# RWKV scan inverse: the power W kept folded to 32 columns, turned folded on VectorE and spread with a block mask

## The reference

```python
def _wkv_step(S, inp):
    r_t, w_t, k_t, v_t, a_t, b_t = inp
    sa = jnp.einsum('zbhvk,zbhk->zbhv', S, a_t)
    S = S * w_t[..., None, :] + sa[..., :, None] * b_t[..., None, :] + v_t[..., :, None] * k_t[..., None, :]
    return S, jnp.einsum('zbhvk,zbhk->zbhv', S, r_t)

def wkv_bidir(state0, scan_in):
    state, ys = lax.scan(_wkv_step, state0, scan_in)
    ys = jnp.moveaxis(ys, 0, 2)
    return state, ys[0] + ys[1][:, ::-1]
```

## Time and profile before

| | us |
|---|---|
| median of 3 runs | 4006.78 (3999.78 to 4009.26) |
| the profiled execution | 4001.04 |
| its span, first to last instruction | 3999.2 |
| products with WR as moving operand, first to last start | 2821.5 to 3349.1 |
| busy in the whole span: PE, PEld, DVE, ACT, POOL | 3689.2, 2635.5, 2316.2, 1210.3, 1289.5 |

### The profile page before, as it was taken

The page is one execution under the profiler, slowest core; times in us unless marked ns, Lnnn a source line. Parts: engine busy times, 40 slices in busy tenths (PEclk is TensorE's granted clock), DMA queues, the critical chain, the costliest instruction groups (busy, mean ns, idle before and its releaser), DMA issues. The chain is left out here.

```text
span 3999.2 us, 76514 instructions
## 1 busy us (share of the span) xinstructions
PE 3689.2 (92%) x30402; PEld 2635.5 (66%) x30402; DVE 2316.2 (58%) x3880; ACT 1210.3 (30%) x2668; POOL 1289.5 (32%) x1004
## 2 busy tenths in 40 slices
PE   8888999898999999899999998898999999899887
PEld 6667778757787798778344444783899997633332
DVE  4568982545986345566344444767777775533333
ACT  3352222344222322332111111224455554111112
POOL 4453445434445355474000000340555552000000
PEclk9999999998999999999999999999999998899999
DMA  4214543302554132234999997255433334599997
GB/s 129 57 54 168 186 155 100 105 1 89 174 182 160 61 106 76 87 131 183 407 420 420 420 420 308 84 186 200 125 91 92 88 96 148 218 376 421 421 421 307
DMA packets 231184, 787.42 MB, mean 197 GB/s; under 512 B 56008, under 2 KB 64024, under 8 KB 171136
## 3 DMA queue, kind: packets, MB, share of 16 engines
q1 hardware_dynamic: 225008, 764.05, 51.4%
q0 software_dynamic: 5328, 19.40, 1.2%
q10 hardware_dynamic: 576, 0.09, 0.0%
HBM read 736.08 MB, written 47.38 MB: 196 GB/s over the span
## 5 line engine op out<-in xcount | busy, mean ns | idle before, releaser
L3011 ACT ACT_TABLE_LOAD x32 | 41.1, 1283 | 519.6 <-PE moe1e_p_u L2957 262.7
L2887 POOL DMA_INDIRECT moe0e_xg<-moe_h,moe_first_rows x20 | 18.9, 947 | 541.1 <-DVE moe_first_rows L3044 535.4
L1227 DVE SCALAR_TENSOR_TENSOR f0u_ada<-hT,condition,f0u_ada 128x512 f32<-128x512 f32 x168 | 189.0, 1195 | 0.4 <-DVE f0u_ada L1227 0.4
L373 POOL TENSOR_TENSOR gmi_w_lo<-gmi_rows_w,gmi_w_hi 128x512 fp32r<-128x512 f32 x64 | 120.2, 1879 | 159.5 <-ACT gmi_w_hi L415 159.5
L1227 DVE SCALAR_TENSOR_TENSOR f1u_ada<-hT,condition,f1u_ada 128x512 f32<-128x512 f32 x168 | 157.8, 1007 | 13.4 <-DMA hT<-in_ada_w_dram 12.9
L4031 PE MATMUL scan_bank<-scan_WR,scan_Z 64*64 64x96 f32 (+1 forms) x3072 | 162.3, 237 | 3.1 <-DVE scan_Z L3949 3.0
L373 POOL TENSOR_TENSOR p_w_lo<-p_rows_w,p_w_hi 128x512 fp32r<-128x512 f32 (+3 forms) x88 | 113.1, 1286 | 160.7 <-ACT p_w_hi L415 160.7
L2887 POOL DMA_INDIRECT moe1e_xg<-moe_h,moe_first_rows x17 | 16.0, 940 | 453.1 <-DVE moe_first_rows L3044 447.4
L1159 POOL TENSOR_TENSOR f0u_w_lo<-f0u_w,f0u_w_hi 128x1024 fp32r<-128x1024 f32 x42 | 114.8, 2754 | 138.0 <-ACT f0u_w_hi L1175 138.0
L1159 POOL TENSOR_TENSOR f1u_w_lo<-f1u_w,f1u_w_hi 128x1024 fp32r<-128x1024 f32 x42 | 113.7, 2726 | 139.1 <-ACT f1u_w_hi L1175 139.1
L2984 PE MATMUL moe0e_p_y<-moe_ring,moe0e_gatedT 128*64 128x512 f32 x608 | 134.7, 594 | 7.8 <-ACT moe0e_gatedT L3013 7.8
(11 more groups left out here) (912 smaller groups left out, 11363.7 us busy)
## 6 DMA issues: line engine op xcount, KB each, us to landing
moe_ring<-in_moe_w_down_dram SPq DMA_DIRECT2D x140, 1024.0 KB, 18.3
gm_uT<-in_moe_w_gu_dram SPq DMA_DIRECT2D x111, 1024.0 KB, 18.0
moe_ring<-in_moe_w_gu_dram SPq DMA_DIRECT2D x102, 1024.0 KB, 21.8
walk_memory<-in_moe_w_gu_dram SPq DMA_DIRECT2D x60, 1024.0 KB, 24.5
hT<-in_ada_w_dram SPq DMA_DIRECT2D x48, 1024.0 KB, 6.8
f0u_w<-in_ffn_w_gate_up_dram SPq DMA_DIRECT2D x22, 1024.0 KB, 4.9
f1u_w<-in_ffn_w_gate_up_dram SPq DMA_DIRECT2D x22, 1024.0 KB, 4.9
gmi_rows_w<-in_ga_w_in_dram SPq DMA_DIRECT2D x64, 256.0 KB, 2.6
```

Source lines behind the costliest of these rows:

```text
L373: nc.gpsimd.tensor_tensor(w_lo[t % 2][:, 0:width], w[t % RAW][:, 0:width], w_hi[t % 2][:, 0:width], ALU.subtract).then_inc(w_lo_made, 1)
L1227: ins = V.scalar_tensor_tensor(out=acc[:, z, :], in0=src, scalar=cond[:, n * HALF + k, z:z + 1], in1=acc[:, z, :], op0=ALU.mult, op1=ALU.add)
L2887: pool.indirect_dma_start(xg[:], None, H.h, bass.IndirectOffsetOnAxis(rows[:, 0:1], 0)).then_inc(gathered, 16)
L3011: nc.scalar.activation(sg[:], p_g[:], ACT.Silu).then_inc(silu_ready, 1)
```

## The change

W is kept folded to 32 columns too. `WR` has now 64 columns per chunk: 32 of W, 32 of the inverse. A new tile `Zt` holds folded powers.

- PE: the nine products of stages 1 to 3 have 64 moving columns and not 96.
- ACT: `copy_power` moves 128 x 128 and not 128 x 256.
- DVE, stage 0: the turn of Z (128 x 256) becomes an add of the two column halves of Z into `Zt` (128 x 128), a wait for it, and a turn of 128 x 128.
- DVE, stages 1 to 3: the turn of the power (128 x 256) becomes a turn of 128 x 128 into `Zt`, a wait for it, and a multiply of `Zt`, read twice, with the block mask, into Z (128 x 256).
- POOL: the same instruction as before, written shorter.

```diff
-        WR = sb("WR", [P, STEPS, CH + CH // 2])
+        WR = sb("WR", [P, STEPS, CH])
+        Zt = sb("Zt", [P, STEPS, CH // 2])
...
-        power, folded = slice(0, CH), slice(CH, CH + CH // 2)
+        power, folded = slice(0, CH // 2), slice(CH // 2, CH)
+
+        def spread(x):
+            return x.rearrange("p c (o t) -> p c o t", o=1).broadcast_to([P, 4, 2, CH // 2])
...
+        block_masks = join[:, 3, :].rearrange("p (q o t) -> p q o t", q=1, o=2).broadcast_to([P, 4, 2, CH // 2])
...
-                        A(WR[:, chunks(n), power], wide(n)[:, :, power], ACT.Copy).then_inc(s["z_copied"], 1)
+                        A(WR[:, chunks(n), power], one(n)[:, :, power], ACT.Copy).then_inc(s["z_copied"], 1)
...
                         if n // NG == FIRST:
                             dve.wait_ge(s["z_copied"], h * COPIED + copies_through(n))
-                            turn(WR[:, g4, power], Z[:, g4, :])
+                            V.tensor_tensor(Zt[:, g4, 0:CH // 2], Z[:, g4, 0:CH // 2], Z[:, g4, CH // 2:CH], ALU.add).then_inc(s["t_half"], 1)
+                            dve.wait_ge(s["t_half"], h * HALVED + n + 1)
+                            turn(WR[:, g4, power], Zt[:, g4, 0:CH // 2])
                         elif squares(n):
-                            turn(Z[:, g4, :], WR[:, g4, power])
+                            V.transpose(Zt[:, g4, :], WR[:, g4, power]).then_inc(s["t_half"], 1)
+                            dve.wait_ge(s["t_half"], h * HALVED + n + 1)
+                            V.tensor_tensor(by_block(Z[:, g4, :]), spread(Zt[:, g4, :]), block_masks, ALU.mult).then_inc(s["t_made"], 1)
...
-                                mm = mmul(wide(n)[:, q], stationary[:, j, :], WR[:, j, :])
+                                mm = mmul(one(n)[:, q, :], stationary[:, j, :], WR[:, j, :])
```

More of the change, by code:

```diff
@@ L3541, in rwkv_scan @@
     NI = PRODUCTS * NG
-    ADDED, COPIED, TURNED = 5 * NG, 5 * NG, 6 * NG
+    ADDED, COPIED, TURNED, HALVED = 5 * NG, 5 * NG, 6 * NG, 4 * NG
     FIRST, LAST_POWER, OUTER, FINAL = 0, 4, 5, 6
@@ L3595, in rwkv_scan @@
                  "tr_ready tr_copied t_made t1_made at_ready "
-                 "off_ready outer_ready inv_ready z_copied r_added r_folded r_full eed_made "
+                 "off_ready outer_ready inv_ready z_copied r_added r_folded r_full t_half eed_made "
                  "bon_ready bon_read bonus_done bonus_shifted km_made kh_made factor_step tables_loaded "
@@ L3618, in one @@
             return bank[INV_BANK[n % 4]][:, 0:4 * CH].rearrange("p (c t) -> p c t", c=4)
-        def wide(n):
-            return bank[INV_BANK[n % 4]][:, 0:4 * (CH + CH // 2)].rearrange("p (c t) -> p c t", c=4)
         def narrow(n):
             return bank[INV_BANK[n % 4]][:, 0:2 * CH].rearrange("p (c t) -> p c t", c=4)
-        power, folded = slice(0, CH), slice(CH, CH + CH // 2)
+        power, folded = slice(0, CH // 2), slice(CH // 2, CH)
+        def spread(x):
+            return x.rearrange("p c (o t) -> p c o t", o=1).broadcast_to([P, 4, 2, CH // 2])
         def by_block(x):
@@ L3759, in body @@
                         pool.wait_ge(s["r_added"], h * ADDED + adds_through(LAST_POWER * NG + g))
-                        nc.gpsimd.tensor_tensor(by_block(full[:, g4, :]), WR[:, g4, folded].rearrange("p c (o t) -> p c o t", o=1).broadcast_to([P, 4, 2, CH // 2]),
-                                                join[:, 3, :].rearrange("p (q o t) -> p q o t", q=1, o=2).broadcast_to([P, 4, 2, CH // 2]), ALU.mult).then_inc(s["r_full"], 1)
+                        nc.gpsimd.tensor_tensor(by_block(full[:, g4, :]), spread(WR[:, g4, folded]), block_masks, ALU.mult).then_inc(s["r_full"], 1)
                     if ahead is not None:
@@ L3961, in add_product @@
                                 dve.wait_ge(s["r_folded"], h * NG + n % NG + 1)
-                            V.tensor_tensor(WR[:, g4, folded], WR[:, g4, folded], wide(n)[:, :, folded], ALU.add).then_inc(s["r_added"], 1)
+                            V.tensor_tensor(WR[:, g4, folded], WR[:, g4, folded], one(n)[:, :, folded], ALU.add).then_inc(s["r_added"], 1)
                         elif n // NG == LAST_POWER:
```

## The result

The changed kernel takes 4026.05 us in the median of 6 runs (4022.98 to 4029.6), against 4005.43 for the kernel before (6 runs, 3999.78 to 4009.26): a ratio of 1.0053, interval 1.0040 to 1.0066. It is 21 us (0.5%) slower, which is small but clear of the interval. The prediction was 4022, with slower as the likeliest outcome.

A forecast was written before the change was run, and what follows sets the result against it. DVE's work on stage 3 was taken to set the tail and the head. 15 heads x 1.04 = 15.6 us on 4001.0 gave 4016.6 profiled, median 4022, own range 4014 to 4032, 8 in 10 3997 to 4037.

The forecast's parts named there:

- The main step: DVE in stages 0 to 3: new two-SBUF-input instructions wait for POOL, so 2.8 us of work costs 1.04 us per head.
- the sum: Whole scan: 15 heads x 1.04 = 15.6 us on 4001.0, giving 4016.6 profiled and a median of 4022.
- The prices: Stages 1 to 3: DVE's cost per unit rises from 0.56 to 0.87 us; copy and half product get shorter.
- idle time before the adds: Sign in the profile: DVE's idle time before adds of stages 1 to 3 falls from 45 to under 15 us.
- The order: Stage 1 to 3 factor parts: `kh` on POOL goes ahead of the second half of `at_rt`, add 6 at 3000.15.
- Rival 1: `at_rt` goes ahead of `kh`: add 7 some 0.6 us earlier, add 12 0.4 late, median 4013; chance 0.20.
- Add 12: DVE's add of product 12, ahead of the tail: at 3007.6 and not 3006.57, making each of 15 heads 1.04 us longer.
- Head 0: First head of the scan: counted among the 15 heads that each get 1.04 us longer.
- The last head: No factor parts, `km` or `kh`: DVE's +0.31 stands against 0.10 + 0.12 off PE and ACT, taken as 0.
- Rival 2: Stages 1 to 3: DVE keeps up, shorter products and copies count, add 12 0.7 us earlier, median 3996; chance 0.15.
- Rival 3: DVE's 128 x 128 turn is all fixed cost, 0.44 us: add 12 2.3 us late, median 4041; chance 0.06.
- Rival 4: The walk sets the head and DVE's delay hides beside it, within 3 us: median 4007; chance 0.12.

The follow-up runs named there:

- experiment 4: Changed kernel with the turned half written to free PSUM columns and the half add taking one half from PSUM: 4005.77 us, ratio 1.0000 to the kernel before.
- Experiment 5: Changed kernel with one more wait on POOL, so `kh` waits until the second half of `at_rt` is done on DVE: 4026.35 us, ratio 1.0048.
- experiments 1: Changed kernel with the products of stages 1 to 3 put back to 96 moving columns: 4030.19 us, ratio 1.0065 to the kernel before.
- Experiment 6: Changed kernel with one idle PE matmul ahead of each wait for a turn of products 10 to 14, heads 0 to 14: 4025.53 us, ratio 1.0047.
- experiment 2: Kernel before with 64-column products in stages 1 to 3 and the 128 x 128 power copy, DVE's work as before, part of W left out: 3997.64 us.
- experiment 3: Changed kernel without the block-mask multiply, the turned half going straight into Z, part of the computation left out: 3991.80 us, ratio 0.9971.

## Why the prediction was right

The main step, that both kinds of new instruction have two inputs in SBUF and so wait for whole POOL instructions, which turns work that would just fit into 1 us more per head, held at each place, and experiment 4 isolates it. Counted from the copy of the bonus, the forecast had adds 3, 6, 8 and 12 at 5.57, 12.57, 15.62 and 20.02 us; they came at 5.61, 12.47, 15.50 and 20.02. In terms of the sum:

- The prices: turn of 128 x 128 0.30, measured 0.302; multiply 0.43 alone, measured 0.425; copy 0.26, measured 0.277; half product 0.23, measured 0.24 (3001.36 to 3001.60); idle time before the adds under 15 us, measured 2.1. One price was missed: a factor part behind a multiply takes 0.03 to 0.04 us longer, from start to start, than one behind a turn (`bh` 0.43 before and 0.47 after, `at_rt` of 128 x 256 0.30 and 0.34, `rk` 0.36 and 0.39). That the chain still ends at 20.02 is partly luck, since the norm's two small ones took 0.34 and not 0.42 and other adds came 0.1 early.
- The order: `kh` went in ahead of `at_rt`, as forecast with a margin of 0.06 us. Rival 1 put a price of 0.6 us on this order. Experiment 5 made that order and won 0.1: a `kh` that starts later also ends later, and the next multiply waits for that end. Since its semaphore itself delays `kh` by up to 0.37 us (0.22 behind against 0.15 ahead), how much of the rival's 0.6 was to be had stays open. The prediction calls this rival the second where it speaks of the order of issue; it is rival 1.
- Add 12 was forecast 1.04 late. It is 1.31 late (18.71 to 20.02). In the head that I read, add 12 already stood 0.28 later than in the others (18.99), which is that difference: in that head it came 1.03 later. The head as a whole got 1.33 longer. 14 x (1.33 - 1.04) = 4 us were missed here.
- Head 0 was counted like the others, 1.0, and got 6.1. It has no walk, and in the trace before DVE has no idle time from its add 3 to its add 12, so that the 2.8 us of added work count in full in that stretch (+3.3), and the half adds with their waits ahead of it (+2.1; with the same DVE work add 3 came 0.7 earlier in the traces of experiments 1 and 6). Experiment 6 puts 1.8 us on its second stretch at the low clock. A full account of the 6.1 was not made. The head was in the trace before: its rows were not looked at.
- The drops of the clock were not foreseen at all. The six heads that they lengthen have 5.7 us more in the profile; with the stalls of either kernel set against each other, 4.3 are left.
- The last head was taken as 0; it gained 0.6.
- The sum was +15.6 us, the profiled spans differ by 21.9 and the medians by 20.6. The 15 heads got 29.0 us longer in the profile, nearly twice the sum: 4.1 more in the quiet part of heads 1 to 14, 5.0 in head 0, 4.3 by drops and stalls. That the spans come within 6.3 of the sum is luck: the part ahead of the scan had 4.4 less in this one profile, and the part behind the last copy 2.7 less.

Rival 2 (PE's and ACT's gain counts) has its size from experiment 2: 0.55 us per head, where I had 0.7, and only while DVE's work does not grow. Rival 3 (turn at 0.44) is out by the turn's 0.302. Rival 4 (the walk hides DVE's delay) is out by the result itself, and experiment 3 shows a head 2.0 us shorter when DVE has less to do.

## What to carry to other kernels

Before an instruction is added on VectorE, ask not only how long it is but whether both its inputs lie in SBUF: then it can wait for the whole of the GpSimd instruction under way, and here 0.43 us became 1.5. If it must be added, try one of its inputs in a free part of PSUM; here that alone gave back the 20 us. Read the first and the last turn of a loop apart from the middle, and read more than one of the middle ones: a stall in the one chosen hid a fifth of the price.

## What the runs showed of the hardware

- A VectorE instruction with one input in PSUM runs in 0.42 us in the midst of a GpSimd instruction that holds back one with two SBUF inputs to 1.50. The turn of 128 x 128 into PSUM takes 0.318, into SBUF 0.302.
- In heads 1 to 14 the granted TensorE clock fell to the 1.2 GHz level for 3 to 4 us at a time, in the head shown behind a stretch in which PE was busy 2.70 of 4.00 us, and five more idle matmuls per head kept it at 2.4 GHz there.
- A half product with 32 x 32 tiles costs 0.36 us for 16 records, with 64 x 64 tiles 0.24 for 8. The small tiles do half the multiplications: they leave out the blocks of zeros, which the large tiles multiply too.
